# First loads of a two-block kernel: the input split in two halves around the first weights, and four projection tiles run in two depth halves

## The reference, cut to what matters

```python
mod = silu(c) @ w_ada[0] + b_ada[0]          # for X and for C: sh1, sc1, g1, sh2, sc2, g2, each 1024 wide
hc = rmsnorm(h_ctx, g_pre_mix[0]) * (1.0 + csc1) + csh1
pc = hc @ w_in[0]                            # 1024 -> 1536, 12 tiles of 128 columns
hx = rmsnorm(x, g_pre_mix[0]) * (1.0 + sc1) + sh1
px = hx @ w_in[0]
```

## Time and profile before

| | us |
|---|---|
| median of 3 runs | 2390.74 |
| lowest and highest run | 2390.58 and 2396.2 |
| the profiled execution, its own time | 2392.48 |
| its span from first to last instruction | 2390.7 |
| PE busy in the span | 2288.5 (96%) |
| DVE, ACT, POOL busy | 807.2, 486.3, 145.8 |

### The profile page before, as it was taken

How to read it: one execution, slowest core, us unless ns; L and a number is a source line. 1 busy time by engine, 2 the same in 40 slices (tenths; PEclk the granted TensorE clock), 3 DMA queues, 4 the chain that set the end, 5 groups by cost and what they waited for, 6 DMA issues and landing times.

```text
span 2390.7 us, 34219 instructions
## 1 busy us (share of the span) xinstructions
PE 2288.5 (96%) x14398; PEld 1674.8 (70%) x14398; DVE 807.2 (34%) x2047; ACT 486.3 (20%) x1144; POOL 145.8 (6%) x150
## 2 busy tenths in 40 slices
PE   6989999999999899999999989999999999999997
PEld 4766888888887678887688845655655555565556
DVE  2245455578433420004665322222222222212223
ACT  3255410000023432101543211111111111111112
POOL 1000111144300000000000000000000000000000
PEclk9999999999999999999999989999999999999999
DMA  8722212133233344344323657999999999999991
GB/s 365 278 103 107 106 71 106 71 139 144 106 141 128 137 182 152 141 163 184 141 106 141 289 225 301 427 426 427 426 426 427 426 427 426 426 427 427 427 425 69
DMA packets 42117, 601.61 MB, mean 252 GB/s; under 512 B 4672, under 2 KB 5184, under 8 KB 5600
## 3 DMA queue, kind: packets, MB, share of 16 engines
q1 hardware_dynamic: 41472, 593.30, 61.2%
q10 hardware_dynamic: 480, 5.97, 0.6%
HBM read 598.20 MB, written 1.05 MB: 251 GB/s over the span
## 4 chain that ended last, share of the span: by engine, by line
PE 84%; DMA 10%; DVE 2%; ACT 2%; issue 1%; POOL 0%; SPq 0%; POOLq 0%; DVEq 0%; PEldq 0%; ACTq 0%
PE PS L1107 15%; PE PS L1131 8%; PE PS L861 8%; PE PS L636 7%; PE PS L671 6%; DMA RG<-in_w_up 6%; PE PS L620 6%; PE PS L723 5%; PE PS L511 4%; PE PS L610 3%; DMA BIG<-in_w_up 3%; PE PS L709 2%; PE PS L1036 2%; PE PS L1143 2%; DMA RG<-in_w_ada 1%; PE PS L451 1%
## 5 line engine op out<-in xcount | busy, mean ns | idle before, releaser
L2400 DVE TENSOR_SCALAR STAT<-PS 128x128 f32<-128x128 f32 (+1 forms) x128 | 37.9, 296 | 668.9 <-PE PS L1107 668.9
L1107 PE MATMUL PS<-BIG,XS 128*64 128x256 f32 (+1 forms) x2016 | 239.3, 388 | 3.4 <-DMA BIG<-in_w_up 3.4
L1107 PEld LDWEIGHTS PS<-BIG,XS 128*64 128x64 f32 (+1 forms) x2016 | 146.7, 139 | 93.8 <-issue 21.5
L1285 ACT ACTIVATE BIG<-PS 128x256 f32<-128x256 f32 (+2 forms) x205 | 85.9, 431 | 500.5 <-PE PS L636 138.9
L1107 PE MATMUL PS<-RG,XS 128*64 128x256 f32 (+1 forms) x1520 | 178.5, 385 | 5.2 <-DMA RG<-in_w_up 5.2
L861 PE MATMUL PS<-XS,RG 128*128 128x256 f32 x768 | 172.1, 382 | 5.0 <-DVE XS L1857 4.1
L861 PEld LDWEIGHTS PS<-XS,RG 128*128 128x128 f32 x768 | 145.7, 192 | 26.6 <-issue 6.9
L1107 PEld LDWEIGHTS PS<-RG,XS 128*64 128x64 f32 (+1 forms) x1520 | 108.3, 138 | 73.6 <-issue 15.6
L1710 ACT ACTIVATE STAT<-STAT 128x128 f32<-128x128 f32 (+1 forms) x128 | 40.1, 313 | 574.1 <-DVE STAT L2400 574.1
L1823 DVE TENSOR_SCALAR HOLD<-PS 128x256 f32<-128x256 f32 x27 | 11.4, 423 | 399.8 <-PE PS L487 299.9
L620 PE MATMUL PS<-HN,RG 128*128 128x256 f32 x640 | 140.6, 382 | 4.0 <-ACT HN L1332 4.0
(11 more groups left out here) (347 smaller groups left out, 3278.7 us busy)
## 6 DMA issues: line engine op xcount, KB each, us to landing
BIG<-in_w_up SPq DMA_DIRECT2D x64, 2048.0 KB, 27.1
RG<-in_w_up SPq DMA_DIRECT2D x48, 2048.0 KB, 27.9
RG<-in_w_ff SPq DMA_DIRECT2D x32, 2048.0 KB, 7.7
BIG<-in_w_down SPq DMA_DIRECT2D x32, 2048.0 KB, 29.2
RG<-in_w_ada SPq DMA_DIRECT2D x24, 2048.0 KB, 7.8
RG<-in_w_down SPq DMA_DIRECT2D x24, 2048.0 KB, 28.7
RG<-in_w_in SPq DMA_DIRECT2D x23, 2048.0 KB, 8.0
SM<-in_w_up SPq DMA_DIRECT2D x16, 2048.0 KB, 27.4
```

The source lines that it names most:

```text
L1107: i = pe.matmul(half_of(b, h, sides), Xg[:, k, 0:cap], w[:, k, h * wd:h * wd + wd], start=False, stop=k == 7)
L1285: i = act.activation(dst, banks[b][rows, part], fn)
```

## The change

The input now comes in two transfers, C's half alone on ACT's queue at the start, X's half on SP's queue behind `w_in` chunk 0. In DRAM the input is laid out stream by stream, so that a half is 8 KB in one piece per partition; the tile in SBUF keeps its layout, so that a half is eight pieces of 1 KB. PE takes the mean of C before ada 3, and transposes each modulation row as soon as it can. The first four tiles of `w_in` are run as eight half tiles: slabs 0 to 3 of tiles 0 to 3, then slabs 4 to 7 of the same tiles into the same four PSUM banks. ada 1's transposes come behind the first half tile, the mean of X behind the second tile's second half. ACT shifts C's slabs 0 to 3 when ada 0's row is there, then copies out ada 1's row and shifts the others; X's squares come only then, X's root behind tile 3, X's shift behind tile 4. DVE reads ada 0's and ada 1's rows right behind C's multiplications, and does X's norm after that.

```diff
             pe.wait_ge(s_cc, 16)
             ada(0, 2)
             pe.wait_ge(s_const, 5)
-            ada(0, 3)
             mean_summed(("mix", 0, C), range(8), own(HN, C), ones)
             ada_turn(0, 2)
+            ada(0, 3)
             ada_turn(0, 3)
-            mean_summed(("mix", 0, X), range(8), own(HN, X), ones)
             ada(0, 0)
+            ada_turn(0, 0)
             ada(0, 1)
-            ada_turn(0, 0)
-            ada_turn(0, 1)
-            for i in range(12):
+            w_in_halves(range(4))
+            for i in range(4, 12):
                 w_in(0, C, i)
...
+            def w_in_halves(tiles):
+                w = chunk(("w_in", 0, C, 0), ("in", 0, C, 3)).rearrange("p (k n) -> p k n", k=8)
+                for half in range(2):
+                    for i in tiles:
+                        b = F.at["in", 0, C, i][0] if half else take(("in", 0, C, i))
+                        for k in range(4 * half, 4 * half + 4):
+                            if i == 0:
+                                pe.wait_ge(s_hn, NORM["mix", 0, C] + k + 1)
+                            m = pe.matmul(banks[b][:, 0:256], w[:, k, 128 * i:128 * i + 128], own(HN, C)[:, k, :],
+                                          start=k == 0, stop=k == 7)
+                        if half:
+                            m.then_inc(s_full[b], 1)
+                        elif i == 0:
+                            ada_turn(0, 1)
+                        if half and i == 1:
+                            mean_summed(("mix", 0, X), range(8), own(HN, X), ones)
...
             def shifted(kind, l, s):
-                if (kind, l) == ("mix", 0):
-                    act.wait_ge(s_mod, ADA[0, 1] + 1)
                 for k in range(8):
+                    if (kind, l, s) == ("mix", 0, C) and k % 4 == 0:
+                        if k:
+                            row(0, 1)
+                        act.wait_ge(s_mod, ADA[0, k // 4] + 1)
...
-            act.dma_start(XS_[:, :], A["xs"]).then_inc(s_in, 16)
+            act.dma_start(own(XS, C), A["xs"][:, C]).then_inc(s_in[C], 16)
...
             squares(0, C, "mix")
-            squares(0, X, "mix")
             row(0, 2)
             root(("mix", 0, C), C)
             row(0, 3)
-            root(("mix", 0, X), X)
             row(0, 0)
-            row(0, 1)
             shifted("mix", 0, C)
+            squares(0, X, "mix")
...
                 if i == 3:
+                    root(("mix", 0, X), X)
+                if i == 4:
                     shifted("mix", 0, X)
...
-            dve.wait_ge(s_in, 16)
+            dve.wait_ge(s_in[C], 16)
             r = {C: rstd(("mix", 0, C), 1e-6, C)}
             turned(0, 2)
             turned(0, 3)
-            r[X] = rstd(("mix", 0, X), 1e-6, X)
             gain(0, 0, 1, "g_pre_mix", 1.0)
             dve.wait_ge(s_coef, 1)
             for s in C, X:
+                if s == X:
+                    turned(0, 0)
+                    turned(0, 1)
+                    dve.wait_ge(s_in[X], 16)
+                    r[X] = rstd(("mix", 0, X), 1e-6, X)
                 for k in range(8):
-                    if (s, k) == (X, 0):
-                        turned(0, 0)
-                    if (s, k) == (X, 4):
-                        turned(0, 1)
...
                 landing(key, source(key))
+                if key == ("w_in", 0, C, 0):
+                    sp.dma_start(own(XS, X), A["xs"][:, X]).then_inc(s_in[X], 16)
...
-    xs = np.concatenate([f["x"][0], f["ctx"][0]], 0)
-    A["xs"] = np.ascontiguousarray(xs.T.reshape(8, 128, 512).transpose(1, 0, 2)).reshape(128, 4096)
+    A["xs"] = np.ascontiguousarray(np.stack([f["x"][0].T.reshape(8, 128, 256), f["ctx"][0].T.reshape(8, 128, 256)]).transpose(2, 0, 1, 3))
```

More of the change, by code:

```diff
@@ L175, in build @@
         s_used = sem("used")
-        s_cc, s_sm, s_in, s_sm2, s_sm3, s_out = (sem(n) for n in ("cc", "sm", "in", "sm2", "sm3", "out"))
+        s_cc, s_sm, s_sm2, s_sm3, s_out = (sem(n) for n in ("cc", "sm", "sm2", "sm3", "out"))
+        s_in = {X: sem("inx"), C: sem("inc")}
         s_const, s_mod, s_coef, s_kz = (sem(n) for n in ("const", "mod", "coef", "kz"))
@@ L496, in w_in @@
                 first = i == (4 if (l, s) == (1, C) else 0)
+                assert (l, s) != (0, C) or i >= 4
                 if i == 5:
@@ L1299, in squares @@
                     if kind == "mix" and l == 0:
-                        act.wait_ge(s_in, 16)
+                        act.wait_ge(s_in[s], 16)
                     else:
```

## The result

In the first measurement, 20 runs of each on one chip, the changed kernel took 2398.67 us (2391.85 to 2402.12) and the kernel before 2390.55 (2384.58 to 2396.7, one run of 3968 left out): a ratio of 1.0029, 95% interval 1.0021 to 1.0038, or 6.9 us (the medians are 8.1 apart). Two later measurements of the same two kernels gave 1.0014 (0.9999 to 1.0029) and 1.0023 (1.0011 to 1.0036): 3.4 and 5.5 us. So the change makes the kernel slower by 3 to 7 us, which is around the 0.3% that the prediction gave as what can be told from no change; in one of the three measurements the interval touches 1. Either kernel scatters over 10 to 14 us from run to run, so a single profile says little about the end; it says much about the start.

What follows compares the result with a forecast made beforehand. PE was taken as the bound, busy 2288.5 of 2390.7 us, so changes come from its idle time or clock. Late tiles +8.9, insertions +1.3, clock -1.8 gave +8.4: 2399.1 us; 8-in-10 range 2385.5 to 2402.

Steps and rivals of the forecast that it cites:

- the tiles start 18.6 after C's landing: Start of the kernel: the steps between C's half landing and the first w_in tile take 18.6 us.
- the path through `w_in` 0: Before the tiles: mean, ada 3, then w_in 0's load, landing at 45.1; the other branch was shorter, 44.0.
- The load's 7.5 after issue: w_in 0's load before the tiles: with its queue empty, it lands 7.5 us after issue, as ada 5 did.
- The -1.8 of the clock: First five tiles: a shorter PE gap avoids the half clock and saves 1.8 us; the other end was 0.
- The insertions of +1.3: Inside the tiles: ada 1's transposes (0.45) and X's mean (0.87), formerly done in idle time, add 1.3 us.
- just in time: After the first tiles: ada 4 lands at 63.6 when PE wants it at 63.5; 1 us may be lost.
- a landing before 9 us: Input load: by the skill's whole-packet rule, C's half needs only a few turns and lands before 9 us.
- Two terms of C's landing: Input load: turns begin at 2.5 us, and pairs cost 0.69 us each, beside ada 2, 3, 0 and 1; landing 26.5.
- the balance point: Start of the kernel: the change gains and loses nothing if C's half lands at 18.1 us.
- the two branches cancel: Rival for the input load: C lands between 15 and 21, total 2388 to 2393 us; chance 0.10.
- the forecast's +8.4: Total shift forecast at ada 4's matmuls and carried unchanged to the end: 8.4 us slower, bounds +5 to +11.
- the prediction's last sign: Whole trace: if the shift at ada 4 is not the shift at the end, carrying it through is wrong.

Runs made afterwards that it cites:

- r8: Changed kernel, but C's half lands as 128 rows of 8 KB in a scratch tile and DVE copies it later; 2390.75 us, 0.9990 of before.
- r3: Changed kernel, but C's half loads on SP's queue, behind the small constants and ahead of ada 2; 2391.61 us, 0.9988 of before.
- r7: Changed kernel, but PE does ada 3 before the mean of C again; 2393.96 us, 1.0004 of before.
- r6: Second measurement of r3's version, C's half first on SP's queue; 2394.03 us, 1.0002 of before.
- r11: r8's version with the rest of the constants issued behind ada 4 instead of behind w_in 1; 2390.80 us, 0.9986 of before.
- r4: Changed kernel, but the input loads whole on ACT's queue as before, the new order and half tiles kept; 2390.98 us, 0.9990 of before.

## Why the prediction was right, and where it was not

**The mechanism was right.** C's half lands late because its short pieces take turns with 16 KB packets; r8 shows it by the pieces' length and r3 by the queue. Ada 3 waits behind the mean, `w_in` 0 behind ada 3, and the tiles behind `w_in` 0; the rule "the tiles start 18.6 after C's landing" gave 36.8 for a landing at 18.2, and it was 37.77. Two steps inside it were off and nearly cancelled: C's mean and ada 2's transposes took 2.8 us (24.27 to 27.10), at half clock, instead of 1.6, and ada 3 took 2.9, 2.2 and 2.1 in the three profiles instead of 3.6. That the path through `w_in` 0 was the longer of two was right by little: r7 took it away and won 1.3. The load's 7.5 after issue was 7.7. The -1.8 of the clock came as forecast: the clock was 1.00 at the tiles in all three profiles. The insertions of +1.3 were 1.3: 0.43 (39.60 to 40.03) and 0.86 (48.67 to 49.53). Ada 4's landing "just in time" cost 0.55 to 0.88.

A short piece cost 0.051 us where 0.057 was taken. Alone on a queue, C's half landed by 7, and the half and the first weights together delayed ada 2 to 11.9 (r3).

The Trainium skill's rule (DMA: Bandwidth & Descriptors, "Queues, rings and completion order"), a whole packet of 9 to 17 descriptors from one ring at a time, does not hold here: 343 packets against 325 in 12 us, with nearly equal counts in each microsecond from 6 on. What the prediction made of that rule, a landing before 9 us, was no fair test of it: it counted the half's own few turns, but not that SP's queue would then hold an engine for several rows of 16 KB, 0.64 us each, in each of its turns. The landing alone would not have refuted the rule; the counts do.

**Two terms of C's landing were mis-sized.** The forecast had the turns begin at 2.5 us, 0.69 each, with all of ada 2, 3, 0 and 1 to get through, and C at 26.5. In fact ada 2's packets began only in the fifth microsecond, though issued at 1.18 and though SP's small rows were through by 3. In the kernel before nobody could see that, since SP's small rows were then still taking turns with the input. By 5 us ACT's queue had moved 43 of each engine's 64 pieces, most of them alone. The other 21 took the 12 us to 17, 0.58 each, below the forecast's 0.61 to 0.69. With 0.58 and the start at 2.5 the forecast's own steps give some 23; the other 4 to 5 us are the head start. So C came at 18.2, which is the balance point that the forecast itself had worked out (18.1), and the case that happened is, by its landing and by its size at ada 4, the one given 0.10: "the two branches cancel".

**The total was right partly by luck.** At ada 4 the four profiles of before have 55.14, 53.63, 54.93 and 54.96, the three of the changed kernel 57.15, 56.74 and 57.16: +2.4 of the forecast's +8.4. At the router the means are 1373.2 and 1374.9, +1.6. At the third expert they are 1479.8 and 1484.0, +4.2. So the prediction's last sign, that a shift at ada 4 that is not the shift at the end speaks against carrying it through, is there. What is added between router and third expert, 2.6 us, is time at half clock: in that stretch the traces have 27.3 us of it in each profile of the changed kernel, and 17.1 and three times 23.9 in those of before. That is 5.1 more on average, and at half pace 5.1 us lose 2.6. The forecast had no such term. It had read the granted clock only in the first tile, and took for granted that a shift at 55 us reaches the end unchanged.

Whose doing the lower clock is stays open, and the record points both ways. In the profiles it goes with the split input: the stretch from router to third expert took 109.0 to 109.3 us in all eight profiles of versions that load the input in halves (the changed kernel, r3, r6, r7, r8, r11), and 104.8 to 107.6 in all five that load it whole (the four of before, r4). But the profiled executions of the changed kernel had a mean clock of 0.985, 0.984 and 0.985, at the low end of its 44 runs (0.983 to 0.993, mean 0.9872). The 81 later runs of before have 0.9885. Of that difference of 0.0013 about 0.0011 is, as an estimate, the longer half clock in the first 60 us (10.2 us in each profile of the changed kernel, 3.4, 3.4, 6.8 and 6.8 in those of before). So the run lists do not show that the changed kernel has the lower clock later on.

The run lists do show that most of the scatter goes with the clock. A straight line through the times of each later session, with one slope for all versions in it, gives 1.2 to 1.4 us for each 0.001 of mean clock. At equal mean clock the changed kernel is then 1.8 and 3.7 us above before (standard error 0.7 and 0.6), or, as an estimate, some 1.4 more with the first 60 us' share of the clock left out. That does not narrow it further.

Of the measured 3.4 to 6.9 us, then, some 2.4 are shown to be the start's. For the rest, up to 4.5, the profiles show time at half clock between router and third expert, and no run shows what brings it about.

## What to carry to other kernels

Here a load on a second queue got one turn for each packet of the first, so that its landing was set by the number of its contiguous pieces and not by its bytes: 1 MB took 17.5 us in pieces of 1 KB and 6.0 in rows of 8 KB. Give what is wanted first either long rows or the first place in the one queue. Before moving a wait ahead of a step in PE's order, ask which loads that step's end releases. And compare landmarks along the whole trace, not ends, and several profiles: in the first pair of profiles two thirds of the effect arose 1300 us after the change.

## What the runs showed of the hardware that was not expected

- A load's first packets can come well after its issue: in the changed kernel ada 2, issued at 1.18, moved nothing until 4.5 us, though the rows ahead of it in its queue were through by 3.2. Of the other versions only r7 has such a gap; in the rest SP's queue still had rows to move ahead of ada 2, so they can't tell whether the 1024 pieces on the other queue are the reason. That stays open.
- The clock column is no guide to PE's pace at the start of a trace: ada 2's 16 matmuls took 3.64 us in the first profile of before, ada 0's and ada 1's 32 together also 3.64, and the column shows 1.00 over both. The trace holds no record of the clock before 22.2 us there, and none before 14 to 17.4 us in the others.
- The same kernel varies by 10 to 14 us from run to run, and mostly with its mean granted clock: in one session the five runs of before at 0.985 average 2399 us, the three at 0.992 average 2387. In the profiles the means over 1365 to 1400 us were either 0.71 to 0.72 or 0.85.
